# A hybrid RWKV-7 and attention block on one core: low-rank products and head sums in two-part form, softmax tiles turned by halves

## What is computed

```python
Pm = P + (shift_right(P, 1) - P) * mu
r, k, v, xw, xa, xg = jnp.split(Pm, cuts, axis=-1)      # 512, 512, 512, 64, 64, 160 columns
w = -jax.nn.softplus(-(w0 + jnp.tanh(xw) @ w_up)) - 0.5
decay = jnp.exp(-jnp.exp(w))
a = jax.nn.sigmoid(a0 + xa @ a_up)
g = jax.nn.sigmoid(xg) @ g_up
kk = k * k_k                                            # per head of 64
kk = kk / jnp.maximum(jnp.linalg.norm(kk, axis=-1, keepdims=True), 1e-12)
k = k * (1.0 + (a - 1.0) * k_a)
...
bonus = jnp.sum(r * k * r_k, axis=-1, keepdims=True) * v
```

## Time and profile before

| | |
|---|---|
| median of 3 runs | 981.47 us |
| the profiled execution's own time | 981.85 us |
| its span, first to last instruction | 979.5 us |
| TensorE busy | 956.0 us, 98% |
| TensorE weight loads | 789.7 us, 81% |
| ScalarE, VectorE, GpSimd busy | 421.7, 398.3, 383.5 us |
| mean granted TensorE clock | 0.998 |
| DMA | 86.43 MB, 88 GB/s |

### The profile page before, as it was taken

How to read it: one execution, slowest core, us unless ns; L and a number is a source line. 1 busy time by engine, 2 the same in 40 slices (tenths; PEclk the granted TensorE clock), 3 DMA queues, 4 the chain that set the end, 5 groups by cost and what they waited for, 6 DMA issues and landing times.

```text
span 979.5 us, 15616 instructions
## 1 busy us (share of the span) xinstructions
PE 956.0 (98%) x6663; PEld 789.7 (81%) x6663; DVE 398.3 (41%) x623; ACT 421.7 (43%) x657; POOL 383.5 (39%) x179
## 2 busy tenths in 40 slices
PE   6999999999999999999999999999999999999996
PEld 4885877787879998888788888888888888888885
DVE  4110258866663456147434434343444310100525
ACT  6244245425556334353345344434443422322656
POOL 2432444433126223334713444444444444435350
PEclk9999999999999999999999999999999999999999
DMA  8441333322211000223612333333233333233132
GB/s 248 116 107 44 87 94 99 84 79 58 62 43 46 4 4 3 73 79 109 234 45 65 87 106 88 107 88 106 88 106 89 105 109 106 86 108 108 64 109 86
DMA packets 115065, 86.43 MB, mean 88 GB/s; under 512 B 2820, under 2 KB 99990, under 8 KB 114998
## 3 DMA queue, kind: packets, MB, share of 16 engines
q1 hardware_dynamic: 114808, 85.37, 29.4%
q10 hardware_dynamic: 190, 0.08, 0.0%
HBM read 83.34 MB, written 2.10 MB: 87 GB/s over the span
## 4 chain that ended last, share of the span: by engine, by line
PE 73%; DVE 2%; ACT 1%; issue 1%; POOL 1%; DVEq 0%; ACTq 0%
PE bank L527 13%; PE bank L529 13%; PE bank L528 13%; PE bank L571 8%; PE bank L573 8%; PE bank L572 8%; PE bank L800 2%; PE bank L810 2%; PE bank L705 1%; PE bank L720 1%; PE bank L693 1%; PE bank L767 1%; PE bank L778 1%; POOL w_lo L507 0%; PE bank L870 0%
## 5 line engine op out<-in xcount | busy, mean ns | idle before, releaser
L507 POOL TENSOR_TENSOR w_lo<-raw,w_hi 128x1024 fp32r<-128x1024 f32 x138 | 333.6, 2417 | 519.3 <-ACT w_hi L1054 519.0
L1054 ACT ACTIVATE w_hi<-raw 128x1024 fp32r<-128x1024 f32 x138 | 146.4, 1061 | 364.9 <-issue 220.3
L527 PE MATMUL bank<-hT_hi,w_hi 128*128 128x512 f32 (+1 forms) x736 | 286.8, 390 | 1.0 <-POOL w_lo L507 0.9
L529 PE MATMUL bank<-hT_hi,w_lo 128*128 128x512 f32 (+1 forms) x736 | 283.2, 385 | 0.0
L528 PE MATMUL bank<-hT_lo,w_hi 128*128 128x512 f32 (+1 forms) x736 | 283.0, 385 | 0.0
L527 PEld LDWEIGHTS bank<-hT_hi,w_hi 128*128 128x128 f32 x736 | 138.3, 188 | 30.0 <-issue 2.1
L529 PEld LDWEIGHTS bank<-hT_hi,w_lo 128*128 128x128 f32 x736 | 138.2, 188 | 27.9
L528 PEld LDWEIGHTS bank<-hT_lo,w_hi 128*128 128x128 f32 x736 | 138.3, 188 | 27.3 <-issue 0.7
L1840 DVE SCALAR_TENSOR_TENSOR cbuf<-bank,params,cbuf 128x511 f32<-128x511 f32 x48 | 36.0, 750 | 133.9 <-ACT cbuf L1387 133.9
L571 PE MATMUL bank<-w_hi,g_hi 128*128 128x512 f32 x184 | 71.7, 389 | 0.0
L573 PE MATMUL bank<-w_hi,g_lo 128*128 128x512 f32 x184 | 71.6, 389 | 0.0
(11 more groups left out here) (260 smaller groups left out, 1288.4 us busy)
## 6 DMA issues: line engine op xcount, KB each, us to landing
raw<-in_w_up_dram SPq DMA_DIRECT2D x48, 512.0 KB, 3.8
raw<-in_w_in_dram SPq DMA_DIRECT2D x33, 512.0 KB, 4.0
raw<-in_w_down_dram SPq DMA_DIRECT2D x24, 512.0 KB, 3.7
raw<-in_w_gate_dram SPq DMA_DIRECT2D x16, 512.0 KB, 3.9
raw<-in_w_out_dram SPq DMA_DIRECT2D x8, 512.0 KB, 4.3
raw<-in_w_ple_gate_dram SPq DMA_DIRECT2D x8, 512.0 KB, 4.1
xs<-in_x_dram SPq DMA_DIRECT2D x4, 512.0 KB, 5.6
raw<-in_w_branch_a_dram SPq DMA_DIRECT2D x4, 512.0 KB, 3.4
```

Source lines behind the costliest of these rows:

```text
L507: nc.gpsimd.tensor_tensor(low(n)[:, :], raw[:, n % RAW_SLOTS, :], high(n)[:, :].bitcast(F32), ALU.subtract).then_inc(*step("pool", ("lo", n)))
L527: nc.tensor.matmul(o, wh, ah, start=first, stop=False)
L529: return nc.tensor.matmul(o, wl, ah, start=False, stop=last)
L1054: nc.scalar.activation(high(u)[:, :], raw[:, u % RAW_SLOTS, :], ACT.Copy) \
```

## The change

- The low-rank products take high and low parts. ScalarE rounds weights and inputs (`lw_hi`, `lx_hi`), GpSimd and VectorE subtract for the low parts, and `lw` and `la` become three products each, written in turn. The last 32 rows of `lg` are stacked three times on 96 rows (`lw_3`, `lx_3`), so that one product does all three; this takes two more DMAs of 64 KB.
- Head sums take a high and a low part of their input (`sum_hi`, `sum_lo`) and a rounded copy of the block of ones. One stands behind each of qk 0 to 7: `kn` behind 0 to 3, `bn` behind 4 to 7.
- VectorE forms keys, key scaling and the bonus product (`keys`) between the shifts of `rw` 8 to 11, ahead of the norms.
- `scores(0)` stands ahead of `v0`, and `transposed_p(0)` and `(1)` between `v0` and `v1`. ScalarE copies `v0` out before it brings in the next unit.
- Softmax tiles with 6 or more blocks are turned by halves: rows 0 to 63 and 64 to 127 of a block each by one transposition into its own bank, for up to 8 blocks; the remaining two of a tile of 10, and tiles of 3, whole.

```diff
-                    sp.dma_start(lora_w[0:32, 2, :], ins["rw_g_up"][0, P:, :]).then_inc(lora_in, 16)
+                    for r in (0, 32, 64):
+                        sp.dma_start(lora_w[r:r + 32, 2, :], ins["rw_g_up"][0, P:, :]).then_inc(lora_in, 16)
...
+                if n == UIDX[("rw", 4)]:
+                    gp.wait_ge(*done("act", "lw_hi"))
+                    nc.gpsimd.tensor_tensor(lw_lo[:, :, :], lora_w[:, 0:2, :], lw_hi[:, :, :].bitcast(F32), ALU.subtract) \
+                        .then_inc(*step("pool", ("lw_lo",)))
...
             pe.wait_ge(cst_in, 16)
-            pe.wait_ge(lora_in, 64)
-            pe.wait_ge(*done("act", "lora_act"))
+            pe.wait_ge(*done("act", "lw_hi"))
+            pe.wait_ge(*done("act", "lx_hi"))
+            pe.wait_ge(*done("pool", "lw_lo"))
+            pe.wait_ge(*done("dve", "lw_lo"))
+            pe.wait_ge(*done("dve", "lx_lo"))
             for i in range(NPAIR):
                 c = slice(i * P, (i + 1) * P)
-                o = begin("lw", i)
-                nc.tensor.matmul(o[:, :], lora_w[0:64, 0, c], lora_x[0:64, 0, :], start=True, stop=True) \
-                    .then_inc(*step("pe", ("lw", i)))
-                o = begin("la", i)
-                nc.tensor.matmul(o[:, :], lora_w[64:128, 0, c], lora_x[64:128, 0, :], start=True, stop=True) \
-                    .then_inc(*step("pe", ("la", i)))
+                ow, oa = begin("lw", i), begin("la", i)
+                for k, (w, x) in enumerate(((lw_hi, lx_hi), (lw_hi, lx_lo), (lw_lo, lx_hi))):
+                    mm = nc.tensor.matmul(ow[:, :], w[0:64, 0, c], x[0:64, 0, :], start=k == 0, stop=k == 2)
+                    if k == 2:
+                        mm.then_inc(*step("pe", ("lw", i)))
+                    mm = nc.tensor.matmul(oa[:, :], w[64:128, 0, c], x[64:128, 0, :], start=k == 0, stop=k == 2)
+                mm.then_inc(*step("pe", ("la", i)))
                 o = begin("lg", i)
-                nc.tensor.matmul(o[:, :], lora_w[:, 1, c], lora_x[:, 1, :], start=True, stop=False)
-                nc.tensor.matmul(o[:, :], lora_w[0:32, 2, c], lora_x[0:32, 2, :], start=False, stop=True) \
+                split3(o[:, :], lw_hi[:, 1, c], lw_lo[:, 1, c], lx_hi[:, 1, :], lx_lo[:, 1, :], True, False)
+                nc.tensor.matmul(o[:, :], lw_3[0:96, c], lx_3[0:96, :], start=False, stop=True) \
                     .then_inc(*step("pe", ("lg", i)))
             for i in range(8, 12):
                 feature_unit(("rw", i), "rw", i)
 
-            def head_sums(tag, src, p):
...
+            def head_sums(tag, p):
+
+                n = p if tag == "kn" else NPAIR + p
+                pe.wait_ge(*done("act", "sum_hi", n))
                 o = begin(tag, p)
-                nc.tensor.matmul(o[:, :], cst("heads"), src, start=True, stop=True).then_inc(*step("pe", (tag, p)))
...
+                nc.tensor.matmul(o[:, :], heads_r[:, :], sum_hi[:, n % 2, :], start=True, stop=False)
+                pe.wait_ge(*done("dve", "sum_lo", n))
+                nc.tensor.matmul(o[:, :], heads_r[:, :], sum_lo[:, n % 2, :], start=False, stop=True) \
+                    .then_inc(*step("pe", (tag, p), ("sum", n)))
...
+                by_half, whole = turned_tiles(n)
+                if by_half:
+                    o = [begin("t", it, "half", q) for q in range(2)]
+                    for x in by_half:
+                        for q in range(2):
+                            mm = nc.tensor.transpose(o[q][:, x * CH:(x + 1) * CH], Sx[half(q), it % 3, x * P:(x + 1) * P],
+                                                     stacked("ident64")[half(q)])
+                    mm.then_inc(*step("pe", ("t", it, "half"), *([] if whole else [("tall", it)])))
+                if whole:
+                    o = begin("t", it, "whole")
+                    for x in whole:
+                        c = (x - whole[0]) * P
+                        mm = nc.tensor.transpose(o[:, c:c + P], Sx[:, it % 3, x * P:(x + 1) * P], ident)
...
+                if i < NPAIR:
+                    head_sums("kn", i)
+                elif i < 2 * NPAIR:
+                    head_sums("bn", i - NPAIR)
+            pe.wait_ge(*done("act", "qk", 10))
+            scores(0)
             token_units([("v0", s) for s in range(4)], [("vt0", m) for m in range(NT)], hT_hi, hT_lo, 2, 512)
-            bonus_sum(NPAIR - 1)
-            pe.wait_ge(*done("act", "qk", 11))
-            scores(0)
+            transposed_p(0)
+            transposed_p(1)
             token_units([("v1", s) for s in range(2)], [("vt1", m) for m in range(NT)], hT_hi, hT_lo, 4, 256)
 
 
@@ -879,9 +904,8 @@
                 mm.then_inc(*step("pe", ("y", c)))
 
             ring.update(any=CHUNK_RING, gate=ATT_GATE, o=ATT_OUT)
-            transposed_p(0)
-            transposed_p(1)
             gate_parts(4)
+            pe.wait_ge(*done("act", "qk", 11))
             scores(1)
...
+            act.wait_ge(lora_in, 16 * 6)
+            nc.scalar.activation(lw_hi[:, :, :], lora_w[:, 0:2, :], ACT.Copy).then_inc(*step("act"))
+            nc.scalar.activation(lw_3[0:96, :], lora_w[0:96, 2, :], ACT.Copy).then_inc(*step("act", ("lw_hi",)))
...
+            nc.scalar.activation(lx_hi[:, :, :], lora_x[:, 0:2, :], ACT.Copy).then_inc(*step("act"))
+            shift_own(4)
+            for r in (0, 64):
+                nc.scalar.activation(lx_3[r:r + 32, :], lora_x[0:32, 2, :], ACT.Copy).then_inc(*step("act", ("lx_hi",)))
...
+                if i < 6:
+                    high_of_sum(i + 2)
+                if i < NPAIR:
+                    norms(i)
+                if i in (4, 5, 7, 9):
+                    decays((4, 5, 7, 9).index(i))
...
-            before(("v1", 0))
+            before(("v0", 0))
+            before(("v0", 1))
             expo(0)
             expo(1)
+            before(("v0", 2))
+            values("vt0", 0, 512, ("v0", 3))
+            before(("v1", 0))
+            flipped_p(0)
+            flipped_p(1)
             before(("v1", 1))
...
+            def low_of_sum(n):
+                dve.wait_ge(*done("act", "sum_hi", n))
+                if n >= 2:
+                    dve.wait_ge(*done("pe", "sum", n - 2))
+                src = squared_keys[:, n % 2, :] if n < NPAIR else bonus[:, n - NPAIR, :]
+                V.tensor_tensor(sum_lo[:, n % 2, :], src, sum_hi[:, n % 2, :].bitcast(F32), ALU.subtract) \
+                    .then_inc(*step("dve", ("sum_lo", n)))
...
-            pre_a(0)
             for p in range(NPAIR):
-                if p + 1 < NPAIR:
-                    pre_a(p + 1)
+                keys(p)
+                if p < 2:
+                    summed_decay(p)
+                shift(8 + p)
+                if p in (1, 2):
+                    low_of_sum(p - 1)
+            for p in range(NPAIR):
+                low_of_sum(p + 2)
                 pre_b(p)
-                if p:
-                    pre_c(p - 1)
-            pre_c(NPAIR - 1)
+            low_of_sum(6)
+            pre_c(0)
+            low_of_sum(7)
+            summed_decay(2)
+            pre_c(1)
+            summed_decay(3)
+            pre_c(2)
+            pre_c(3)
 
...
+def turned_tiles(n):
+
+    return (range(0), range(n)) if n < 4 else (range(min(n, 8)), range(8, n))
+
...
```

154 lines of the change are left out of this document (93 added, 61 removed).

## The result

The kernel after takes 970.15 us (median of 969.92, 970.32, 974.25 and 969.98), the one before 981.65 us (median of 4 runs beside it, 980.55 to 982.2). The ratio is 0.9896, interval 0.9883 to 0.9909: faster by 1%. The forecast was 968.1 us, range 964 to 973. The profiled execution of the kernel after took 969.92 us (span 968.1, mean granted clock 0.997), 11.93 less than that of before; the sum had said 13.4.

The account below looks back on a forecast made before the run. The prediction took TensorE, busy 956.0 of 979.5 us, as the bound. Gains of 5.7, 3.5, 2.7 and 1.5 sum to 13.4 us, taking 981.85 to 968.4, set at 968.1 us for the runs' median; range 964 to 973.

Parts of the forecast that it names:

- The bound: Whole kernel: TensorE, busy 956.0 of 979.5 us, sets the end, so nearly every microsecond taken off it comes off the end.
- The low-rank products: Stretch after the last `rw` product: fp32r products in place of plain float32, 12.75 to 7.1 us, a gain of 5.7 us.
- Rival 1: Low-rank products: the fp32r halves run one after the other, gain 2.9 us instead of 5.7, 970.9 us; 10%.
- the 8 seams: Low-rank products: changes between 128-row and 64-row products, charged 0.09 us each, 0.7 us in all.
- The head sums: Behind qk 0 to 7: two fp32r products, 0.454 us, replace 0.89 us a sum; a gain of 3.5 us for eight.
- Rivals 3 and 4: Head sums: VectorE late, TensorE waits 3 to 4 us, 971.6 us, 8%; TensorE at VectorE's pace from first, 985.8 us, 3%.
- The waits around `v1`: Around `v1`: TensorE's waits of 1.13 and 1.56 us for ScalarE's copies of `vtok` go, a gain of 2.7 us.
- Rival 2: The waits come back at `scores(1)` or before `v1`: 2.7 us more, 970.8 us; 9%.
- Turning by halves: Softmax tiles: 88 blocks, about 11 groups of 8, gain 0.14 us a group, 1.5 us in all.
- Rival 5: Softmax tiles: each block by halves pays a second weight load of 0.108 us, 9.5 us added, 979.1 us; 3%.
- changes nothing in count: Around `v1`: moving `scores(0)` and the transpositions was itself said to change nothing in count.

Follow-up runs that it names:

- control: The kernel after measured again unchanged on the same chip: 970.15 us, ratio 0.9892 against the kernel before.
- grouped: Against the kernel after, all four `lw`/`la` groups come first, then the four `lg` groups: 970.93 us, ratio 0.9898 against the kernel before.
- one after the other: Against the kernel after, the three `lw` products, then the three `la` products, not alternating: 970.93 us, ratio 0.9891 against the kernel before.

## Why the prediction was right, and its sizes not

**The bound** was right: TensorE sets the end, and time taken off it arrives there. Each stage's gain in the table stands to TensorE's last products, except 0.55.

**The low-rank products: mechanism right, size off.** 4.67 us, not 5.7; plain float32 put back costs 4.7. Rival 1 is excluded: the fp32r halves start together. The wrong term is the charge for "the 8 seams", 0.09 each. I read only the interval into a 64-row product (77.16 to 77.48) in the earlier trace rows, and took that for the whole cost of a change. The trace of the kernel before had the other side as well, one row further on than the earlier trace rows go:

```profile
90.48 0.40 PE L528 MATMUL bank<-hT_lo,w_hi 128*128 128x512 f32 x1
```

That is 0.34 us behind the first full-height product at 90.14, where 0.23 is usual. So the cost is paid on the interval behind the first product of the new height too, 16 times in the stretch and not 8: 28 x 0.227 + 16 x 0.1 = 8.0. Grouping, which leaves two changes, took 0.57 off with a wait and 1.2 without one (8.08 to 6.85).

**The head sums: right.** 3.5 us forecast, 8 x (0.89 - 0.454); the copies stand 5.89 apart and plain sums cost 3.63 more. Rivals 3 and 4 did not happen, since VectorE kept its lead. I had expected 4 us or more, and it was 6. The meetings with GpSimd that I had feared did happen, 1.1 to 1.3 us in each of three low parts, 1.4 and 2.2 in multiplications; they did not come in every step. With 14.3 us more on VectorE the waits appear and the kernel takes 10.9 us more, so their mechanism exists, and only its condition failed.

**The waits around `v1`: right.** 2.7 us; 3.1 of waits come back when the order is undone. Rival 2 did not occur.

**Turning by halves: mechanism right, size off.** 0.8 us (table, and tiles put back whole), not 1.5. The term was 0.14 us for each of 11 groups, with a seam of 0.09 already taken off. The blocks of a group of 8 did gain about what the earlier trace rows promised, 0.14 to 0.15 (0.79 to 0.65 or 0.64), but that is before the seam. Measured from the start of the last product ahead of a group to the start of the second product behind it, the gain is this:

| group, ahead of it | before | after | gain | groups |
|---|---|---|---|---|
| 6 blocks, a product of 128 rows | 1.12 | 1.17 | -0.05 | 2 |
| 8 blocks, a product of 128 rows | 1.34 | 1.30 | 0.04 | 2 |
| 10 blocks, a product of 128 rows | 1.56 | 1.48 | 0.08 | 2 |
| 6 blocks, scores (from the first score) | 2.87 | 2.93 | -0.06 | 2 |
| 8 blocks, scores | 3.51 | 3.41 | 0.10 | 2 |
| 10 blocks, scores | 2.25 | 1.88 | 0.37 | 1 |
| 10 blocks, weighted values (from their first) | 3.28 | 3.05 | 0.23 | 1 |

The twelve add up to 0.8. By the earlier trace rows and its own seam the prediction had 0.79 - 0.64 - 0.09 = 0.06 for a group of 8, and it took 0.14, from the middle of a span that reached up to 0.26. That choice failed, and the seam was a little too small as well: it costs 0.09 ahead of a group (0.32 for 0.23) and 0.03 behind (0.34 for 0.31, since the interval behind whole blocks was a long one already). The groups of 6 lose 0.2 in all, and those of 10 make most of the gain. The groups behind scores are no clean case, since scores have 64 rows too: from the first score to the first transposition the next round of `scores(1)` takes 2.07 us (218.87 to 220.94), before 1.92 (230.39 to 232.31), with no change of height between them. That cause is open. Leaving the tiles of 6 whole would by these rows save another 0.2 us, an estimate; it was not run.

Rival 5, the second load of 0.108 us, is excluded: 16 loads and products take 0.65 us. So the rule it rested on (the Trainium skill, page "TensorE: Matmul & The Clock Gate", section "LDWEIGHTS (loading the stationary operand)") does not hold here for loads of 64 rows and 128 columns: 41 ns each, and 81 ns even if the two halves of a block are counted as side by side.

**Missed altogether:** the wait at L853, 0.63 us, which the prediction put at nothing. I had counted the bank give-outs around `v1` only for `v1` itself. Moving two give-outs from one ring to another shifts the phase of all that follow in it; the step "changes nothing in count" was true of products and false of banks.

The account: 13.4 - 1.0 (seams) - 0.7 (halves) - 0.6 (bank) + 0.4 (a start that was earlier by chance, the control's differs too) + 0.3 (the stage of head sums and `v1`) = 11.8, and the traces differ by 11.78 at their last marked product. Of the 0.3, 0.11 is the long interval at 90.14 to 90.48, which is 0.23 now (85.08 to 85.31); for the rest I have no cause. The spans differ by 11.4 and the executions by 11.93. Behind TensorE's last product 0.3 us of the lead are lost, and what follows is not in the account at all: outside the span lie 2.2 to 2.6 us in every run of the kernel before beside the experiments and 1.8 to 1.9 in every run of the changed kernels, so about half a microsecond is gained where no row shows it, and why is open. The forecast thus came as near as 2 us partly by luck: its terms, as measured, and the wait it missed give 11.1 (13.4 - 1.0 - 0.7 - 0.6), and the early start and the shorter rest outside the span, which it had not counted, made up for some of that.

**Still open:** runs of about 4 us more. Of kernels with the wait at L853, 8 of 33 runs lie 2 to 5 us above their others (the kernel after 1 of 4, its control 1 of 5, grouped 1 of 4, one after the other 1 of 4, whole tiles 2 of 5, plain low-rank products 2 of 6, plain sums 0 of 5; the two with long waits elsewhere are left out). These eight have a mean granted clock of 0.993 or 0.994, the other 25 of 0.996 to 0.998. Of the four kernels without it, none of 16, and none of the 50 runs of the kernel before. Of the nine profiled executions that have the wait, the clock fell right behind it in two, each time for some 10 us and with 3.9 us lost, which is the size of the long runs; in the seven others it stayed at 1.00. That the wait sets it off is likely by these counts, and not shown by them: there is no experiment in which only the length of the wait changed.

## What to carry to other kernels

On a TensorE-bound kernel, price an edit by the distance between starts, and read a seam on both of its sides before it is multiplied. Compare stages rather than whole spans: here the start alone moved the end by up to 1 us. Where buffers are given out in turn, count what an edit does to the turn: a stage 140 us later can meet another reader, and it costs one line to put the phase back. When an operation is put on the path of an engine with slack, say how much lead it has in us; then a test that eats the lead shows where it ends.
